# Level queries of a scan in four tails per slot, one GpSimd instruction per head

## The reference

```
bc     = cumsum(logf) inside a chunk
scores = einsum('bhtk,bhsk,bhtsk->bhts', q, k, exp(bt[t] - bt[s]))   # s <= t
o      = scores @ v + (q * exp(bt)) @ state
state  = exp(b_last) * state + (k * exp(b_last - bt))^T @ v
o_r    = o_forward + o_backward, then a root-mean-square norm per head
```

## Time and profile before

| what | value |
|---|---|
| median of three runs | 3474.61 us (3471.65 to 3475.27) |
| profiled execution, span from the first to the last instruction | 3475.4 us |
| TensorE matmul busy | 3315.4 us, 95% |
| VectorE busy | 2112.2 us, 61% |
| GpSimd busy | 1588.7 us, 46% |
| ScalarE busy | 969.1 us, 28% |
| mean granted TensorE clock | 0.979 of full speed |

### The profile page before, as it was taken

The page is one execution under the profiler, slowest core; times in us unless marked ns, Lnnn a source line. Parts: engine busy times, 40 slices in busy tenths (PEclk is TensorE's granted clock), DMA queues, the critical chain, the costliest instruction groups (busy, mean ns, idle before and its releaser), DMA issues.

```text
span 3475.4 us, 44870 instructions
## 1 busy us (share of the span) xinstructions
PE 3315.4 (95%) x16138; PEld 2538.4 (73%) x16138; DVE 2112.2 (61%) x3509; ACT 969.1 (28%) x2203; POOL 1588.7 (46%) x1534
## 2 busy tenths in 40 slices
PE   8989999999999999999999988999999987899998
PEld 5665555555557967888888756688888865678887
DVE  7577756544544296555646668478764776656554
ACT  2076211001021174211122264222213244332211
POOL 1054322222235224444454467456645547655654
PEclk9999999999999999999999989999999998999999
DMA  7300223333312201345432200244443200022222
GB/s 254 130 10 7 97 98 120 104 122 114 107 58 73 79 2 37 122 158 170 158 96 85 64 12 11 85 156 158 153 143 99 86 28 18 12 88 88 88 89 79
DMA packets 91129, 317.87 MB, mean 91 GB/s; under 512 B 10816, under 2 KB 13152, under 8 KB 90912
## 3 DMA queue, kind: packets, MB, share of 16 engines
q1 hardware_dynamic: 64224, 218.34, 19.5%
q10 hardware_dynamic: 24768, 90.19, 7.1%
q0 software_dynamic: 1920, 6.49, 0.7%
HBM read 312.88 MB, written 2.10 MB: 91 GB/s over the span
## 4 chain that ended last, share of the span: by engine, by line
PE 86%; DVE 7%; ACT 3%; POOL 2%; issue 2%; DMA 0%; DVEq 0%; ACTq 0%; SPq 0%; POOLq 0%
PE ps L1336 66%; PE ps L1338 4%; PE ps L631 3%; PE ps L1293 2%; PE ps L1006 1%; PE ps L1246 1%; PE ps L992 1%; PE ps L1028 1%; PE ps L1189 1%; DVE arena L2626 1%; PE ps L1231 1%; PE ps L1064 1%; ACT arena L1520 1%; DVE arena L2584 1%; PE ps L1261 1%
## 5 line engine op out<-in xcount | busy, mean ns | idle before, releaser
L1336 PE MATMUL ps<-arena 128*128 128x256 f32 (+1 forms) x3744 | 952.4, 408 | 0.2
L1336 PEld LDWEIGHTS ps<-arena 128*128 128x128 f32 x3744 | 710.8, 190 | 204.9 <-issue 1.7
L2757 POOL TENSOR_TENSOR arena<-ring,arena 128x512 f32<-128x512 f32 (+1 forms) x140 | 182.6, 1304 | 836.8 <-PE ps L1336 836.8
L1336 PE MATMUL ps<-arena,ring 128*128 128x256 f32 (+1 forms) x2032 | 524.9, 410 | 3.1 <-ACT arena L1690 3.1
L1336 PE MATMUL ps<-hbuf,ring 128*128 128x256 f32 (+1 forms) x1824 | 469.4, 407 | 4.2 <-ACT hbuf L1797 1.2
L1336 PEld LDWEIGHTS ps<-arena,ring 128*128 128x128 f32 x2032 | 385.3, 190 | 119.5 <-ACT arena L1690 5.9
L1336 PEld LDWEIGHTS ps<-hbuf,ring 128*128 128x128 f32 x1824 | 345.8, 192 | 113.7 <-ACT hbuf L1797 19.5
L2300 DVE TENSOR_TENSOR arena<-ps,arena 128x256 f32<-128x256 f32 (+1 forms) x192 | 86.1, 449 | 356.7 <-PE ps L1336 235.6
L2187 DVE CUSTOM_DVE_ANT_0 aring<-aring,csil,adab 128x1024 f32<-128x1024 f32 x176 | 261.7, 1508 | 1.8
L2305 DVE SCALAR_TENSOR_TENSOR resid<-ps,mod,resid 128x256 f32<-128x256 f32 (+2 forms) x296 | 137.4, 482 | 185.2 <-PE ps L1336 180.5
L2740 POOL TENSOR_TENSOR arena<-ring 128x512 f32<-128x512 f32 (+1 forms) x140 | 182.1, 1301 | 141.2 <-PE ps L1336 133.6
(11 more groups left out here) (324 smaller groups left out, 5342.3 us busy)
## 6 DMA issues: line engine op xcount, KB each, us to landing
aring<-in_ada ACTq DMA_DIRECT2D x172, 512.0 KB, 4.7
ring<-in_mlp SPq DMA_DIRECT2D x128, 512.0 KB, 3.7
ring<-in_up SPq DMA_DIRECT2D x88, 512.0 KB, 3.3
ring<-in_in SPq DMA_DIRECT2D x56, 512.0 KB, 3.3
ring<-in_down SPq DMA_DIRECT2D x32, 512.0 KB, 3.6
ring<-in_odd_in SPq DMA_DIRECT2D x24, 512.0 KB, 3.3
arena<-in_ada SPq DMA_DIRECT2D x16, 512.0 KB, 13.7
ring<-in_out SPq DMA_DIRECT2D x16, 512.0 KB, 3.3
```

The lines of the kernel that those rows point to most:

```text
L1336: return nc.tensor.matmul(ps[:, bank, 0:p.tw], w, x, start=start, stop=stop, skip_group_check=True)
L2757: nc.gpsimd.tensor_tensor(s[3], f0[:, h:2 * h], s[1], ALU.subtract).then_inc(wsum_ready, 1)
```

## The change

A slot becomes a quarter of the width of four consecutive rows in place of the whole width of two: one tile in each of four tails, so the four tiles of a slot lie at an even spacing of 768 columns. Slots 0 to 3 stay in X and 4 to 7 in H; two slots share four rows, one in columns 512 to 639 and one in 640 to 767. With even spacing one instruction of GpSimd covers the four tiles of a head, 64 partitions by 4 x 64 elements, where two covered two tiles each. The matmul's operand takes the new index; it reads the same shape. Signals and waits are as before: the last instruction of a level signals `query_ready`.

```diff
         def level_queries(v):
 
             k = v % 8
-            return (X, H)[k // 4][:, 2 * (k % 4):2 * (k % 4) + 2, S:T]
+            j = k % 4
+            return (X, H)[k // 4][:, 4 * (j // 2):4 * (j // 2) + 4, S + P * (j % 2):S + P * (j % 2) + P]
...
                                 mm = nc.tensor.matmul(ps[:, 2 + v % 2, t * P:(t + 1) * P], WL[:, 7 * (1 - d) + li, t * P:(t + 1) * P],
-                                                      level_queries(v)[:, t // 2, t % 2 * P:(t % 2 + 1) * P], start=True, stop=True)
+                                                      level_queries(v)[:, t, :], start=True, stop=True)
...
-                            dst = level_queries(v).rearrange("p a (c h b m) -> p a h c b m", c=2, h=2, m=m)
+                            dst = level_queries(v).rearrange("p t (h b m) -> p h t b m", h=2, m=m)
                             for hx in range(2):
                                 rows = slice(64 * hx, 64 * hx + 64)
-                                for half in range(2):
-                                    x = nc.gpsimd.tensor_tensor(dst[rows, half, hx], w[rows, 2 * half:2 * half + 2],
-                                                                q[rows, 2 * half:2 * half + 2], ALU.mult)
+                                x = nc.gpsimd.tensor_tensor(dst[rows, hx], w[rows], q[rows], ALU.mult)
                             x.then_inc(query_ready, 1)
```

## The result

Each kernel was run 20 times. The changed kernel takes 3482.80 us (3477.34 to 3490.87), the kernel before 3476.47 us (3469.47 to 3483.36); the ratio is 1.0020, with a 95% interval of 1.0014 to 1.0027. I had forecast 3471.3 us and a range of 3463 to 3479. The change makes the kernel slower by some 6.3 us, and it was forecast faster by 3.3.

What follows compares the result with a forecast made beforehand. TensorE holds 86% of the chain, GpSimd 2%, its queries only in unit 0. Unit 0's 1.95 us less 0.3 in unit 1 gives 1.65 per scan, -3.3 for two: 3471.3 us, range 3463 to 3479.

Steps and rivals of the forecast that it cites:

- The price, 0.72 us for 64x256: GpSimd's query instruction of 64x256 was to take 0.72 us, with 0.675 as low end and 0.994 as high end.
- the pitch, 1.57: Time per level of GpSimd's queries alone: 1.57 us instead of 1.87, and 1.79 for m = 1 and 2.
- Unit 0, -1.95 us: First of a scan's six units: faster queries end its last merge 1.95 us sooner, at 2077.1 instead of 2079.07.
- rival 3: Unit 0's gain is hidden because TensorE stays at 1.2 GHz one or two levels longer: 3474.6 to 3476 us; chance 0.13.
- my cap: In unit 0, TensorE at half clock sets levels 0 to 2, so a query price of 0.675 would add hardly anything.
- The holds, 0.53 and 0.64 for 64x256, two speeds of VectorE: Unit 1: each query holds VectorE 0.53 or 0.64 us; steps 0.87 beside GpSimd, 0.335 after; window grows by 0.3.
- Rival 1: Each 64x256 query holds VectorE for its full 0.72 us (0.83 for m = 1, 2): 3480.3 us; chance 0.08.
- Unit 3, 0 +- 0.2 us: VectorE's window in unit 3, beside GpSimd: same holds in sum, so a change of 0 +- 0.2 us.
- The added early parts: GpSimd's 512-wide adds come sooner behind unit 1, may be shut out by VectorE's stream, and cost nothing.

Runs made afterwards that it cites:

- run 20: Not a follow-up run: part of "Each kernel was run 20 times", the number of timed runs of each kernel.
- e4_pause: Changed kernel, with GpSimd stopped in units 1 and 3 ahead of level 4 until VectorE has issued the next unit's wide products: 3459.69 us, ratio 0.9955.

## Why the prediction was wrong

Its steps, one by one:

- **The price, 0.72 us for 64x256.** Right: 0.717. So was the pitch, 1.57 (1.59), and the level with m = 1 or 2, 0.83 (0.835 in unit 0).
- **Unit 0, -1.95 us.** The size was right, -2.08 and -2.09, and rival 3 did not come in; the reason that I gave for it was not. I had TensorE cap the gain, with 2.07 us for each of levels 0 to 2 at the half clock. It ran them back to back at the half clock (granted clock 0.50 until 2071.5, 0.81 from there to 2074.5), but that goes faster than a level alone: levels 0 to 3 took 6.39 us together, where my prices give 7.4 (3 x 2.07 + 1.17). So TensorE had caught up by level 4, it waited for GpSimd before the last two levels, and the chain stays on GpSimd to the last query. GpSimd's own gain, 14.24 to 12.15 us, was passed on whole; that my cap came out so near to it is luck.

```profile
2067.36 6.39 PE L1247 MATMUL ps<-resid,arena 128*128 128x128 f32 x32 [2.96 <-POOL resid L2927]
...
2075.80 1.13 PE L1247 MATMUL ps<-hbuf,arena 128*128 128x128 f32 x8 [0.30 <-POOL hbuf L2927]
2077.32 1.16 PE L1247 MATMUL ps<-hbuf,arena 128*128 128x128 f32 x8 [0.40 <-POOL hbuf L2927]
```

- **The holds, 0.53 and 0.64 for 64x256, two speeds of VectorE.** Right: steps of 0.87 and 0.98 beside the queries. With the adds held back the window was 15.1 between the chain's marks (2079.97 to 2095.05), where I had 14.8: it grew by 0.6 and not 0.3, since VectorE met twelve queries and not eleven. Rival 1, a hold of the instruction's full length, would be steps of 1.06. The Trainium skill's rule of an exclusive lock (SBUF — State Buffer, "SBUF: two separate sides") agrees with the trace as to the blocking, but not as to "the whole instruction": holds of 0.265, 0.535 and 1.07 us stand beside instructions of 0.444, 0.717 and 1.26, each 0.18 to 0.19 less.
- **Unit 3, 0 +- 0.2 us.** Without the adds right: 15.27 against 15.17.
- **"The added early parts ... come sooner behind unit 1 and may be shut out by VectorE's stream ... so that costs nothing."** This is the step that failed, and with it the sign. I followed the adds only as victims: whether their lateness would hurt somebody. I did not ask what they would do to VectorE in a window that I had just worked out hold by hold. They are two-input GpSimd instructions like the queries, each with four times the elements per partition of a 64x128 one, and the second of them, the sum of the keys, the prediction doesn't name at all. Before, GpSimd was so slow that its last query in unit 1 ended 0.7 us after VectorE's window, and the adds missed the window. (In unit 3 the first add began 1.1 us before the first merge, at 2139.78. It ran there beside a VectorE product that reads PSUM, whose step was 0.60 us with the add beside it and 0.60 without.) The gain on GpSimd (12 instructions at a step of 0.87 to 0.98 in place of 24 at 0.60 to 0.66) made it end 6.9 us before the first merge, and 2 x 1.07 us of holds went into each of four windows: +8.6 us, against a gain of 3.0. The rest of the two scans' 6.6 us lies in merges and in the units that TensorE sets, where its clock differs.
- **The evidence I used for it.** The 5.61 us of the earlier trace rows was a lone add that arrived from a wait in the middle of VectorE's running stream. The adds in question follow GpSimd's own stream within 0.1 us, and a GpSimd stream that is running kept every second turn in all windows here. It was not even a rule for lone adds: in the second scan of e4_pause (GpSimd's timeline and VectorE's below) the same add arrived in the middle of VectorE's key products and went through in 1.30 us. What decides there stays open.

```profile
2880.96 1.30 POOL L2961 TENSOR_TENSOR resid<-resid,junk 128x512 f32<-128x512 f32 x1 [3.29 <-ACT junk L1922]
```
```profile
2879.37 4.04 DVE L2608 TENSOR_TENSOR arena<-arena 128x256 f32<-128x256 f32 x7 [7.24 <-ACT arena L1870]
```

- **TensorE's clock.** Its idle time in unit 1 went from 2.6 us (2092.31 to 2094.90) to 7.0 (2090.84 to 2097.88), and the three levels after it had a granted clock of 0.50 where it was 0.64, shown by these windows of before and after (length, busy us of PE, PEld, DVE, ACT, POOL, clock). The merges of the first scan's unit 1 took 0.8 us more. The other merges of units 1 and 3 took from 0.85 us less to 0.5 more, so no sum is to be made of it.

```profile
2094.90:2099.60 4.70, 4.68 (x24) 4.29 (x24) 2.80 (x6) 3.00 (x11) 4.41 (x8) 0.64 0.00 0
```
```profile
2097.90:2103.40 5.50, 5.44 (x24) 5.15 (x24) 2.78 (x7) 3.31 (x11) 4.56 (x6) 0.50 0.00 0
```

The sum for the first scan, from the starts and ends behind the table: -2.1 in unit 0, +2.8 in window 1, +0.8 in its merges, +2.3 in window 3, +0.5 in its merges, and -1.5 in the units that TensorE sets: +2.8. In units 4 and 5, which hold most of the last term, the order is unchanged and TensorE's granted clock fell at other moments (its mean over these units was 0.92 before and 0.96 after); in the second scan the same units took 1.4 us more, with 0.96 before and 0.92 after. So I take that term for scatter of the clock.

## What to carry to other kernels

When an engine off the critical path gets faster, list everything in its queue up to its next wait, place it at the new time, and ask which engine works there and whether the two hold each other up. Each two-input GpSimd instruction here held a two-input VectorE step up by its own duration less 0.18 to 0.19 us, and merging the instructions did not change that sum much. Where VectorE is on the chain, it can pay to make GpSimd wait for the end of the run, with only what is needed next let in (here 0.45% with the changed instruction, 0.53% with unit 0 as well), until another engine sets the time. And a faster instruction may be worth little where it is hidden and much once the order leaves it on the path: the same change was +6 us in the one order and -9 in the one with the stop.

## What the runs showed of the hardware

- Beside VectorE's two-input float32 products (steps of 0.335 us for 256 elements), a stream of GpSimd products got one instruction per VectorE step in these windows, whatever its length: steps of 0.60, 0.87 and 1.41 us with GpSimd's 128, 256 and 512 elements.
- GpSimd's two-input instructions lie near one line whether on 64 or 128 partitions: 0.444 and 0.717 us for 128 and 256 elements on 64, 0.99 and 1.26 for 384 and 512 on 128, about 2.1 ns per element beside 0.17. The row of 128x256 in the earlier trace rows, 0.675, lies 0.04 below it; why is open. With every second float in the inputs (m = 1), or every second pair (m = 2), 128 and 256 elements took 0.50 and 0.83.
- The same adds beside VectorE's merges, which read PSUM, held them up by nothing that can be seen: 2.72 us for two levels with them, 2.70 without.
- TensorE's level of eight matmul records took 2.07 us alone at the granted clock of 0.50; three such levels in a row, with a fourth at the risen clock, took 6.39.
